# Rounded probabilities written by a second exponential on ScalarE, and high-part products of both heads first, in the frames attention of an encoder kernel

## The reference, cut to what matters

```
def _mla_attend(q_lat, q_rope, ckv, kr, mask):
    s = (einsum('bqhl,bkl->bhqk', q_lat, ckv) + einsum('bqhr,bkr->bhqk', q_rope, kr)) * MLA_SCALE
    ...
    p = jax.nn.softmax(s, axis=-1)
    return einsum('bhqk,bkl->bqhl', p, ckv)

def _swa_attend(q, k, v, sinks, key_mask):
    s = einsum('...qkgd,...skd->...kgqs', q, k) * SWA_SCALE
    ...
    p = jax.nn.softmax(concatenate([s, sink], axis=-1), axis=-1)[..., :-1]
    o = einsum('...kgqs,...skd->...qkgd', p, v)
```

## Time and profile before

| | us |
|---|---|
| median of 3 runs | 3059.45 |
| lowest and highest | 3054.79, 3065.43 |
| span of the profiled execution | 3057.4 |
| stage B of the first layer | 216 to 500 |
| stage B of the second layer | 1714 to 2008 |

### The profile page before, as it was taken

One profiled execution on the slowest core, in us unless ns is written; L12 is line 12 of the kernel. 1 busy time (PEld: TensorE's weight loads), 2 busy tenths in 40 slices (PEclk: granted clock), 3 DMA queues, 4 the chain that ended last, 5 costly groups with the idle time before them and its releaser, 6 DMA issues.

```text
span 3057.4 us, 54602 instructions
## 1 busy us (share of the span) xinstructions
PE 2900.7 (95%) x20464; PEld 2641.8 (86%) x20464; DVE 2153.7 (70%) x3903; ACT 1256.5 (41%) x2474; POOL 1728.5 (57%) x1388
## 2 busy tenths in 40 slices
PE   7989998999999999999989899989999999999997
PEld 6966666887999999999989666668889999999997
DVE  6767777657776767778755677776577777678777
ACT  3334434435344434444333344444454444344442
POOL 2323333436777767888632233333377777678875
PEclk9989998999999999999989899989999999999998
DMA  4321114653333343333322211155432333433331
GB/s 168 134 87 41 54 37 139 179 167 107 103 109 111 108 157 139 105 104 111 131 93 97 87 42 42 36 173 180 150 116 94 108 110 107 183 111 114 101 104 57
DMA packets 193137, 336.06 MB, mean 110 GB/s; under 512 B 57200, under 2 KB 112752, under 8 KB 190800
## 3 DMA queue, kind: packets, MB, share of 16 engines
q1 hardware_dynamic: 166528, 276.94, 28.1%
q10 hardware_dynamic: 17248, 30.28, 2.7%
q0 software_dynamic: 9136, 25.89, 2.2%
HBM read 263.48 MB, written 65.52 MB: 108 GB/s over the span
## 4 chain that ended last, share of the span: by engine, by line
PE 80%; DVE 9%; issue 3%; ACT 2%; DMA 2%; POOL 2%; SPq 0%; POOLq 0%; DVEq 0%; ACTq 0%
PE PS L2966 23%; PE PS L2968 22%; PE PS L2967 22%; PE PS L3093 5%; DVE mxc L2464 1%; POOL Pl L1555 1%; PE PS L3361 1%; DMA winraw<-in_W_IN 1%; PE PS L3254 1%; PE PS L2986 1%; DMA ht<-in_X 1%; ACT Pf L1873 1%; PE PS L3398 0%; PE PS L3344 0%; PE PS L3140 0%
## 5 line engine op out<-in xcount | busy, mean ns | idle before, releaser
L1608 POOL TENSOR_TENSOR wopl<-T,woph 128x512 fp32r<-128x512 f32 x348 | 524.0, 1525 | 98.6 <-ACT woph L2064 97.5
L1555 POOL TENSOR_TENSOR Pl<-Pf,Ph 128x256 fp32r<-128x256 f32 (+5 forms) x174 | 219.0, 1266 | 370.1 <-DVE Ph L2503 370.1
L2966 PE MATMUL PS<-hidh,wdh 128*128 128x320 f32 (+1 forms) x1408 | 418.9, 298 | 5.5 <-DVE hidl L2780 4.4
L2968 PE MATMUL PS<-hidh,wdl 128*128 128x320 f32 (+1 forms) x1408 | 418.9, 298 | 0.0
L2967 PE MATMUL PS<-hidl,wdh 128*128 128x320 f32 (+1 forms) x1408 | 417.9, 297 | 0.0
L2064 ACT ACTIVATE woph<-T 128x512 fp32r<-128x512 f32 x348 | 216.6, 630 | 477.0 <-DVE T L2775 260.8
L2966 PE MATMUL PS<-xoh,woph 128*128 128x320 f32 x1232 | 382.6, 311 | 3.5 <-POOL wopl L1608 3.0
L2968 PE MATMUL PS<-xoh,wopl 128*128 128x320 f32 x1232 | 381.1, 309 | 0.0
L2967 PE MATMUL PS<-xol,woph 128*128 128x320 f32 x1232 | 380.1, 309 | 0.0
L2833 DVE TENSOR_TENSOR acc<-acc,PS 128x320 f32<-128x320 f32 (+1 forms) x608 | 275.5, 455 | 148.3 <-PE PS L2968 145.3
L2966 PE MATMUL PS<-x_both,woph 128*128 128x264 f32 x1232 | 350.2, 284 | 0.0
(11 more groups left out here) (498 smaller groups left out, 7840.7 us busy)
## 6 DMA issues: line engine op xcount, KB each, us to landing
ru<-in_W_FF SPq DMA_DIRECT2D x88, 512.0 KB, 4.2
rd<-in_W_FF SPq DMA_DIRECT2D x176, 256.0 KB, 2.7
rg<-in_W_FF SPq DMA_DIRECT2D x82, 512.0 KB, 4.2
xs_scratch<-x_part ACTq DMA_DIRECT2D x56, 264.0 KB, 2.5
x_both<-xs_scratch ACTq DMA_DIRECT2D x14, 1056.0 KB, 7.6
sqt_scratch<-sqTs POOLq DMA_DIRECT2D x18, 512.0 KB, 4.6
hc<-out_H SPq DMA_DIRECT2D x18, 512.0 KB, 3.7
dkraw<-in_CKVT SPq DMA_DIRECT2D x16, 520.0 KB, 4.5
```

Of the source, the lines that this page charges most:

```text
L1555: ins = pool.tensor_tensor(Pl[i][0:kk, 1, c], Pf[i][0:kk, 1, c], f(Ph[i][0:kk, 1, c]), ALU.subtract)
L1608: pool.tensor_tensor(wopl[k][:, :, :], w_whole(w, k, first), f(woph[k][:, :, :]), ALU.subtract)\
L2966: pe.matmul(out, wh, mh, start=start, stop=False)
L2968: return pe.matmul(out, wl, mh, start=False, stop=stop)
```

## The change

Three edits, all in stage B.

- ACT computes each exponential twice from the same PSUM slot: first into `Ph`, rounded as it is written (`b_ph`), then into `Pf` (`b_exp`, as before). Both stand at the entry `st`.
- DVE no longer casts `Pf` into `Ph`. Its subtraction for the even head and POOL's for the odd one both wait for `b_exp`.
- PE's `pv` is put in another order. After `b_ph` come the products with `Ph` of both heads, then after `b_sp_even` and `b_sp_odd` the products with `Pl`. The products and their number are the same.

```
@@ frames, POOL, sp
-                        pool.wait_ge(S("b_sp_hi"), F(l, "sp", n) + 1)
+                        pool.wait_ge(S("b_exp"), F(l, "st", n) + 1)
@@ frames, ACT, st
+                        for kk, c in prob_parts(u):
+                            ins = act.activation(Ph[r][0:kk, :, c], both_banks(u)[0:kk, :, c], ACT.Exp)
+                        ins.then_inc(S("b_ph"), 1)
                         for kk, c in prob_parts(u):
                             ins = act.activation(Pf[r][0:kk, :, c], both_banks(u)[0:kk, :, c], ACT.Exp)
                         ins.then_inc(S("b_exp"), 1)
@@ frames, DVE, sp
-                        for kk, c in prob_parts(STEPS[n]):
-                            ins = dve.tensor_copy(Ph[r][0:kk, :, c], Pf[r][0:kk, :, c])
-                        ins.then_inc(S("b_sp_hi"), 1)
-                        dve.wait_ge(S("b_sp_hi"), q + 1)
@@ frames, PE, pv
+                        begins, ends = st["first"] or st["which"] == "W", st["last"] or st["which"] == "W"
+                        pe.wait_ge(S("b_ph"), F(l, "st", n) + 1)
+                        for h in range(2):
+                            for e, (kk, out, c, vh, vl) in enumerate(parts_of(h)):
+                                pe.matmul(out, vh, Ph[r][0:kk, h, c], start=begins and e == 0, stop=False)
+                                pe.matmul(out, vl, Ph[r][0:kk, h, c], start=False, stop=False)
                         for h in range(2):
                             pe.wait_ge(S("b_sp_odd" if h else "b_sp_even"), F(l, "sp", n) + 1)
...
+                            last = parts_of(h)
+                            for e, (kk, out, c, vh, vl) in enumerate(last):
+                                ins = pe.matmul(out, vh, Pl[r][0:kk, h, c], start=False, stop=ends and e == len(last) - 1)
                         ins.then_inc(S("b_pv"), 1)
```

More of the change, by code:

```diff
@@ L3230, in frames_pe, with parts_of @@
                                 pe.wait_ge(S("b_item_lo"), by_dve(l, ITEM["vh", st["j"] // 2]))
-                        for h in range(2):
-                            pe.wait_ge(S("b_sp_odd" if h else "b_sp_even"), F(l, "sp", n) + 1)
+                        def parts_of(h):
                             if st["which"] == "M":
@@ L3236, in frames_pe @@
                                 c = slice(c0, BANK)
[L3237 to L3246, removed]
+                                return [(kk, acc_bank(h)[0:V66, c], c, VHh[b][0:kk, st["k"], h, :], VHl[b][0:kk, st["k"], h, :])]
+                            out = acc_bank(h)[0:V66, 256 * st["k"]:256 * st["k"] + 256]
+                            return [(block[3], out, slice(band_at(block), band_at(block) + 256),
+                                     band_values(0, h, block), band_values(1, h, block))
+                                    for block in swa_blocks(st["j"], st["k"])]
+                        begins, ends = st["first"] or st["which"] == "W", st["last"] or st["which"] == "W"
[4 more added lines that the diff above has]
+                                pe.matmul(out, vl, Ph[r][0:kk, h, c], start=False, stop=False)
+                        for h in range(2):
+                            pe.wait_ge(S("b_sp_odd" if h else "b_sp_even"), F(l, "sp", n) + 1)
+                            last = parts_of(h)
+                            for e, (kk, out, c, vh, vl) in enumerate(last):
+                                ins = pe.matmul(out, vh, Pl[r][0:kk, h, c], start=False, stop=ends and e == len(last) - 1)
                         ins.then_inc(S("b_pv"), 1)
```

## The result

The changed kernel takes 3107.6 us (median of 5 runs, 3101.1 to 3109.1) beside 3055.7 us for the kernel before on the same chip: ratio 1.0155, 95% interval 1.0141 to 1.0170. The predicted time was 3098.5 us in a range of 3074 to 3124.

The account below looks back on a forecast made before the run. The prediction took PE as the bound, slightly held up by low parts and ACT. Per layer 20.1 us lost less 3.8 won gives 16.3; 33 for both plus 6 of clock, added to 3059.5, makes 3098.5 us, range 3074 to 3124.

Parts of the forecast that it names:

- The places: Spots in stage B where PE waits on ACT's slots or queue; doubled exponentials there lose 20.1 us per layer.
- the clock: Stages B: more standing still lowers TensorE's mean clock by about 0.02, costing 6 us for both layers.
- The exponential's price: ACT in stage B: the 174 added exponentials take the present durations, 751 ns on average, bounded to 1%.
- (a): Hand-over W to M, 4 times per layer: PE waits longer for ACT's `QR`; 1.4 us each, 5.6.
- (b): Second M step with `sx`, 3 times per layer: the doubled exponential holds a needed slot; 1.4 us each, 4.2.
- (d): Turned queries, 4 times per layer: an exponential ahead of `QR` delays it; 0.64 us each, 2.6.
- (c): First M step with four `sx`, 3 times per layer: PE waits for ACT's last exponential; 1.7 us each, 5.1.
- The signs named for the waits: PE's wait at hand-overs for `QR` about 2.8 us (from 1.64); before the third `sx` 2 or more (from 0.66).
- the pv waits: Four pv near the end of the 9-step pass stop waiting for low parts, winning 1.1 us per cycle.
- The full clock rival: Stages B: half speed follows each hand-over pause; means fall 0.05 or more, 28 us, so 3120 us; chance 0.09.
- The winning chain: Stage B: ACT's slack covers the doubling, only removed waits count, near 18 us, so 3041 us; chance 0.06.
- The draw: Stage B: stalls hide in each other's shadow and relieved DVE helps, returning 33 of 40 us; 3062 us; chance 0.07.

Follow-up runs that it names:

- x_places: New product order, with the second exponential only in 32 of 72 steps of a layer and DVE's cast in the others; 1.0153 against the kernel before.
- x_sbuf: Full change, but ACT computes one exponential into `Pf` and copies it from SBUF into `Ph`, freeing the PSUM slot earlier; 1.0087 against the kernel before.
- x_keep: Full change, but DVE still casts after the second exponential and all wait for its cast; 1.0186 against the kernel before.
- x_warm2: Full change plus PE products of no use, sized to its pauses (9 at hand-overs into 9-step passes, 5, 4); 1.0087 against the kernel before.
- x_warm: Full change plus PE products of no use before waits for ACT (9 at every W-to-M hand-over, 7, 5); 1.0164 against the kernel before.

## Why the prediction was right, step by step

**Direction and mechanism.** Right. The places were named, and x_places shows that they carry the loss. The split of the loss between slots and queue was about half and half; x_sbuf took 21 us of 48 away. The size came out nearer than its terms: waiting was put at 33 us and measured 25, the clock was put at 6 and costs about 22. The two errors have opposite signs, and that 39 came within 9 us of 48 is in part luck.

**The exponential's price.** 1025 ns were assumed for one into fp32r, and the trace after has a mean of 1025 ns for 128x1024. Right as a length. What one adds to ACT's queue is 0.92 us, for the next begins 0.1 us before its end, and the sums at the places did not take this off.

**Places.** (a) 1.25 us against 1.4, (b) 0.9 against 1.4, (d) 0.4 against 0.64 were somewhat too high. (c) was too low: 2.4 against 1.7. Its row shows PE's wait 1.6 us longer, close to the 1.7; the other 0.8 us come between the pause and the second M step, whose scores are already computed at half speed (0.63 us for a pair of products). So the wait at (c) was right, and what it lacked was the clock. Over the cycle these errors cancel: without the clock at `mx` I had 4.1 us and the starts give 4.3 (6.2 less 1.9), with the 0.8 us of clock at (c) in them. The signs named for the waits came as said or nearly: 2.60 us for `QR` (2.8 expected) and 2.24 us before the third `sx` (2 or more).

**Gains.** 1.1 us per cycle for the pv waits, measured 1.2. For the two layers I had 7.6 us; the runs give 6 for the order and 9 for the cast. The second is more than my walk found, though its interval does not exclude a few us less. In x_keep the low parts come behind two exponentials and the cast, and PE still waits for them. That the cast is worth more beside the longer exponential than in the kernel before, so that the two terms are not independent, would fit this; no run separates it.

**The clock.** The term that was mis-sized. I took the mean clock to fall by 0.02 and 6 us to come of it. Within the stages B it fell by 0.04 in each layer, half speed grew by 51 us, and PE's busy time and x_warm2 put the price at 20 to 22 us. The full clock rival (0.05, 28 us) was nearer in its clock and somewhat too high in its price. It also had the wrong place: I had expected half speed behind the hand-overs with their longer pause, and had counted five such in the first layer before. The clock record before has four stretches there (from 241, 313, 385 and 484 us); three begin 3 us behind the wait for the turned queries, (d), and none begins within 10 us behind a hand-over. After, half speed comes behind every (c) and every (d), where two pauses (2.24 and 1.31 us) lie 12 us apart, and at two of the eight hand-overs, where PE waits for 2.60 us. Why it comes at the one and seldom at the other is not shown here.

**The rivals.** The winning chain is out by the 60.0 us of waits for ACT. The draw is out too: the stalls added up in nearly every row of the table, and no 33 us came back. The rule on a saturated DVE (the Trainium skill, Perfetto Trace Analysis, section Optimizing Scalar/DVE Operations) was not tested by this kernel, whose DVE is not saturated (72% of the stage): with DVE relieved by 57 us in a stage, the gain from it was about 9 us in all.

## What to carry to other kernels

An engine that is idle for 60% of a stage may still be the last to finish at its seams: look for the rows in which the bound engine waits for it, before its idle time is spent. Doubling an instruction there costs nearly its full length per seam (0.9 of 1.02 us at the second M step), and where the pauses that it makes are followed by half speed of TensorE, it may cost that much again: here 25 us of waiting and 22 us of slower products. Where work is moved, move it only in the steps behind which there is cover; 20 of 72 steps were free here, 32 carried everything.

## What the runs showed of the hardware

POOL's subtraction became shorter though it was not touched. In the first layer's stage B, before and after:

```profile
L1555 POOL TENSOR_TENSOR Pl<-Pf,Ph 128x512 fp32r<-128x512 f32 x24 | 42.5, 1770 | 49.0 <-DVE Ph L2503 49.0
```

```profile
L1555 POOL TENSOR_TENSOR Pl<-Pf,Ph 128x512 fp32r<-128x512 f32 x23 | 31.1, 1350 | 75.6 <-ACT Pf L1876 75.6
```

Before, DVE's subtraction from the same tiles began 0.045 us ahead of it, and POOL's row is longer by 0.42 us on average: 46 of the 48 instructions of this shape take 1.78 to 1.81 us. After, DVE mostly comes later, and 40 of 48 take 1.27 to 1.30. It works the other way too. At 510.89 us in the kernel after, DVE's subtraction of 128x512 began 0.34 us behind POOL's and took 1.79 us, the longest of its line, where such a one takes 0.68 when POOL is not at work; it ended 0.54 us behind POOL's.

```profile
L2506 DVE TENSOR_TENSOR Pl<-Pf,Ph x174: 280/547/1785, 224.9 to 2057.1; 128x512 fp32r<-128x512 f32 x48, 128x256 fp32r<-128x256 f32 x44, 80x256 fp32r<-80x256 f32 x32, 16x512 fp32r<-16x512 f32 x16
```

Of the three numbers in nanoseconds, the last is the longest. The Trainium skill says in SBUF — State Buffer, section SBUF: two separate sides, that a DVE instruction with two SBUF inputs and a GpSimd one that reads SBUF exclude each other for their whole length. The trace agrees in kind: the one that comes second is longer by most of the other's length, by 0.5 us for POOL (1.79 less 1.28, DVE's being 0.69) and by 1.1 us for DVE (1.79 less 0.68, with 1.24 of POOL's left).

Products of no use, put mostly where TensorE would stand still anyway, took its granted clock in stage B from 0.93 and 0.92 to 0.99 and 0.98 and won 20 us, though they compute nothing (x_warm2). With more of them, and more where there was no pause, they cost all that they won (x_warm).
